# Second attention: scores from stacked high and low halves that transfers put in place

## What is computed

```python
def rmsnorm(x, g):
    xf = x.astype(jnp.float32)
    y = xf * lax.rsqrt(jnp.mean(xf * xf, axis=-1, keepdims=True) + EPS)
    return (y * g.astype(jnp.float32)).astype(x.dtype)
...
def window_attention(q, k, v, k_ctx, v_ctx, sink, scale):
...
        s_ctx = jnp.einsum('bqkgd,bckd->bkgqc', qi, k_ctx).astype(jnp.float32) * scale
        s_win = jnp.einsum('bqkgd,bskd->bkgqs', qi, ki).astype(jnp.float32) * scale
        s_win = jnp.where(valid, s_win, NEG_INF)
        p = jax.nn.softmax(jnp.concatenate([s_ctx, s_win, sink_col], axis=-1), axis=-1).astype(v.dtype)
        return (jnp.einsum('bkgqc,bckd->bqkgd', p[..., :n_ctx], v_ctx)
                + jnp.einsum('bkgqs,bskd->bqkgd', p[..., n_ctx:n_ctx + span], vi))
...
    k_ctx, v_ctx = gqa_keys_values(h_ctx, k_g)
    k_lat, v_lat = gqa_keys_values(h_lat, k_g)
    q_lat = apply_rope(gqa_queries(h_lat, q_g), cos, sin).reshape(B, L, C_KV_HEADS, C_GROUP, C_HDIM)
    k_lat = apply_rope(k_lat, cos, sin)
    o_lat = window_attention(q_lat, k_lat, v_lat, k_ctx, v_ctx, sink, scale)
```

## Time and profile before

| what | value |
|---|---|
| median of 3 runs | 3370.38 us (3369.05 to 3371.79) |
| the profiled execution | 3368.63 us, of which the span is 3366.8 us |
| TensorE busy | 3128.4 us (93%), 14506 instructions |
| VectorE, ScalarE, GpSimd busy | 1618.1 us, 1043.6 us, 472.2 us |
| mean granted clock of TensorE | 0.967 |
| second attention | 2192 to 2513 us of the span |

### The profile page before, as it was taken

How to read it: one execution, slowest core, us unless ns; L and a number is a source line. 1 busy time by engine, 2 the same in 40 slices (tenths; PEclk the granted TensorE clock), 3 DMA queues, 4 the chain that set the end, 5 groups by cost and what they waited for, 6 DMA issues and landing times. The chain is left out here.

```text
span 3366.8 us, 38293 instructions
## 1 busy us (share of the span) xinstructions
PE 3128.4 (93%) x14506; PEld 2220.9 (66%) x14506; DVE 1618.1 (48%) x2027; ACT 1043.6 (31%) x1435; POOL 472.2 (14%) x375
## 2 busy tenths in 40 slices
PE   5987999999897999999999969879989899999998
PEld 2552444444586888888888847734438688888887
DVE  4123555565326555555555462255633555555554
ACT  3014566556413111111111130035552312222221
POOL 0003554555300000000000000035440000000000
PEclk9987999999898999999999989979999899999999
DMA  9800000000201111111111001000000211111111
GB/s 384 328 36 17 4 4 3 2 3 0 94 19 70 38 35 35 36 35 34 36 35 37 25 13 50 25 16 1 1 20 31 76 38 44 62 44 44 44 62 50
DMA packets 34912, 162.28 MB, mean 48 GB/s; under 512 B 3890, under 2 KB 6706, under 8 KB 24755
## 3 DMA queue, kind: packets, MB, share of 16 engines
q1 hardware_dynamic: 34834, 161.24, 13.4%
HBM read 157.03 MB, written 4.19 MB: 48 GB/s over the span
## 5 line engine op out<-in xcount | busy, mean ns | idle before, releaser
L716 PE MATMUL PS<-f_uh,f_Wh 128*128 128x512 f32 (+1 forms) x1760 | 483.4, 372 | 25.2 <-DVE f_ul L453 24.2
L716 PE MATMUL PS<-f_ul,f_Wh 128*128 128x512 f32 (+1 forms) x1760 | 481.7, 371 | 0.0
L716 PE MATMUL PS<-f_uh,f_Wl 128*128 128x512 f32 (+1 forms) x1760 | 480.9, 371 | 0.0
L866 DVE SCALAR_TENSOR_TENSOR X<-PS,mod,X 128x512 f32<-128x512 f32 (+1 forms) x440 | 306.3, 698 | 309.1 <-PE PS L716 308.9
L716 PEld LDWEIGHTS PS<-f_uh,f_Wh 128*128 128x128 f32 x1760 | 307.8, 188 | 89.6 <-issue 19.4
L716 PE MATMUL PS<-f_gh,f_WDh 128*128 128x512 f32 (+1 forms) x880 | 330.8, 376 | 19.4 <-DVE f_gl L852 17.2
L716 PEld LDWEIGHTS PS<-f_ul,f_Wh 128*128 128x128 f32 x1760 | 308.8, 188 | 59.1
L716 PEld LDWEIGHTS PS<-f_uh,f_Wl 128*128 128x128 f32 x1760 | 308.4, 188 | 59.0
L716 PE MATMUL PS<-f_gl,f_WDh 128*128 128x512 f32 (+1 forms) x880 | 325.8, 370 | 0.0
L716 PE MATMUL PS<-f_gh,f_WDl 128*128 128x512 f32 (+1 forms) x880 | 325.7, 370 | 0.0
L835 DVE SCALAR_TENSOR_TENSOR part<-PS,part,part 128x1023 f32<-128x1023 f32 (+1 forms) x132 | 130.0, 1013 | 328.6 <-ACT part L771 328.5
(11 more groups left out here) (268 smaller groups left out, 4601.0 us busy)
## 6 DMA issues: line engine op xcount, KB each, us to landing
part<-in_mod_w SPq DMA_DIRECT2D x48, 1024.0 KB, 7.3
part<-in_w_up SPq DMA_DIRECT2D x88, 512.0 KB, 3.5
part<-in_w_down SPq DMA_DIRECT2D x22, 1024.0 KB, 5.5
part<-in_w_out SPq DMA_DIRECT2D x16, 512.0 KB, 3.5
X<-in_xT SPq DMA_DIRECT2D x4, 1280.0 KB, 10.2
...
```

What stands on the lines that cost most here:

```text
L716: mm = pe.matmul(ps(bank + c, hi - lo), w_, x_[:, lo:hi], start=f_, stop=l_)
L866: dve.scalar_tensor_tensor(out=X[:, m, lo:hi], in0=ps(DNB[r % 2], hi - lo), scalar=moda(layer, 5, m, 0 if lo < SEQ else 1), in1=X[:, m, lo ...
```

## The change

The score product becomes two float32r products into the same bank. `ks` holds the low half of K on the upper 64 partitions and the high half on the lower, `qh` the high half of Q twice, so one pass gives low K with high Q and high K with high Q. `kh` (high K, with the row of ones) times `ql` (low Q, with the row of the maximum) is the second.

VectorE now writes a finished piece over all 128 rows in place into its PSUM bank (L2274; for the context piece one operation, L2262, with no rotation product and no `turn`). In the pair after, ScalarE copies it to a stage as float32r, its high half (`high`, L2155), VectorE subtracts to the low half (`low`, L2282), GpSimd casts the high half to bfloat16 after its addition (L1963), and SyncE moves the parts to their partitions: four transfers of the high half, two of bfloat16, two of the low half for a full piece. The first three pieces and the rest have stages of their own: `high` and `low` wait for the transfers of all pieces before from the fifth piece on, since those share one stage. Squares of the first four pieces use two buffers. Four buffers for queries take the place of six. The zero fills of the bfloat16 tiles go from VectorE to GpSimd, the rotation table comes in four transfers, and TensorE no longer waits for it. Pieces and early maxima stand at other pairs, and upfront the steps of neighbouring pieces interlock.

```diff
-            qa = [[take(SEQ) for _ in range(C_GROUP)] for _ in range(2)]
-            ka = [take(T) for _ in range(2)]
-            pr = [take(2, BANK) for _ in range(3)]
-            osb = take(BANK)
-            acc = [take(SEQ) for _ in range(2)]
-            rope = take(2, T)
-            qb = [take(SEQ // 2).bitcast(BF16) for _ in range(C_GROUP)]
-            kb = [take(T // 2).bitcast(BF16) for _ in range(2)]
-            es = take(SEQ)
-            sq = [take(BANK) for _ in range(2)]
-            lnr = take(BANK)
...
-            t1, lnb = X[:, 0:2, SEQ:T], X[:, 2:4, SEQ:T]
...
+            QS = 4
+            qh, ql = halves("qh", QS, SEQ), halves("ql", QS, SEQ)
+            at_pr = [take(2, BANK) for _ in range(3)]
+            pr = [big(x, 2, BANK) for x in at_pr]
+            rope = [plain(SEQ), MIX1[:, 5, :]]
+            ks, kh = halves("ks", 2, T), halves("kh", 2, T)
+            acc = [plain(SEQ) for _ in range(2)]
+            qb = [plain(SEQ // 2).bitcast(BF16) for _ in range(C_GROUP)]
+            kb = [plain(T // 2).bitcast(BF16) for _ in range(2)]
...
+            sq = [QK1[:, 1:4:2, SEQ:T], acc[1][:, 0:BANK].rearrange("p (a b) -> p a b", b=CTX)]
+            early_b = [acc[0][:, 256 * n:256 * n + 256].bitcast(BF16) for n in range(3)]
+            stages = [(place("h1_stage_h", take(2, CTX), 2, CTX),
+                       place("h1_stage_l", O_QK1, KT, T)[:, 5:8:2, SEQ:T])]
+            for b in range(3):
+                stages.append([place(f"h1_stage_{kind}{b}", at_pr[b] + n * BANK, 2, CTX) for n, kind in enumerate("hl")])
+            t1, lnb, osb = [X[:, 2 * b:2 * b + 2, SEQ:T] for b in range(3)]
+            stage_b = X[:, 6, SEQ:T].bitcast(BF16)
...
+                at(pair - 1, 1 if pair > 1 else 0, "tn", G, w)
                 at(pair, 0, "nt", G, w)
                 at(pair, 1, "ro", G, w)
-                at(pair + 1, 0, "ca", G, w)
+                at(pair + 1, 0, "hi", G, w)
+                at(pair + 1, 1, "lo", G, w)
+                at(pair + 1, 1, "ca", G, w)
+
+            def upfront(n):
+
+                for kind, w in [("sq", 0), ("nt", 0), ("tn", 0)] + [(kind, w + d) for w in range(n) for kind, d in (
+                        ("ro", 0), ("sq", 1), ("nt", 1), ("tn", 1), ("hi", 0), ("lo", 0), ("ca", 0)) if w + d < n]:
+                    at(UPFRONT, 0, kind, 0, w)
...
-            EARLY = [(0, 0), (0, 1), (1, 0), (1, 1), (2, 0), (2, 1), (3, 0), (4, 0)]
+            EARLY = [(0, 0), (0, 1), (1, 0), (1, 1), (2, 1), (3, 0), (3, 1), (4, 0)]
...
-                for w, r in enumerate((-15, -13, -9, -7, -3)):
-                    product(o + r if G else 1 if w == 4 else UPFRONT - 1, G, w)
+                if G == 0:
+                    upfront(NW - 1)
+                    product(0, G, NW - 1)
+                else:
+                    for w, r in enumerate((-15, -13, -10, -7, -3) if G == 1 else (-19, -15, -13, -7, -3)):
+                        product(o + r, G, w)
...
+                def moves(G, w):
+
+                    t_, c = prods[w]
+                    b, lo, hi = G % 2, *CH[c]
+                    top, bottom = slice(0, 64), slice(64, P)
+                    first, second = [], []
+
+                    def query(j, rows_):
+                        n = queries(G, j)
+                        first.extend((qh[n][half, lo:hi], rows_) for half in (top, bottom))
+                        second.append((ql[n][top, lo:hi], rows_))
+                    if t_ == 0:
+                        first.extend(((ks[b][bottom, lo:hi], bottom), (kh[b][top, lo:hi], bottom)))
+                        second.append((ks[b][top, lo:hi], bottom))
+                        if c < 2:
+                            query(2, top)
+                    else:
+                        query(0, top)
+                        query(1, bottom)
+                    return first, second
...
+                def staged(G, w):
+
+                    return stages[w + 1 if G == 0 and w < 3 else 0]
...
+                def before(q):
+
+                    return 0 if q < 4 else q
...
+                    sp.wait_ge(s["one"], 2 + QS)
+                    for G in range(C_KV):
+                        for w in range(NW):
+                            q = NW * G + w
+                            m = CH[prods[w][1]][1] - CH[prods[w][1]][0]
+                            at_least(sp, "S", 2 * NU * (C_GROUP * G + (-3 if w < 3 else -1)))
+                            first, second = moves(G, w)
+                            stage_h, stage_l = staged(G, w)
+                            sp.wait_ge(s["hi"], q + 1)
+                            for dst, rows_ in first:
+                                sp.dma_start(in_halves(dst).bitcast(F32), halved(stage_h[rows_], m).bitcast(F32))\
+                                    .then_inc(s["moved"], 16)
+                            sp.wait_ge(s["cast"], q + 1)
+                            sp.wait_ge(s["pad"], 2 + C_GROUP)
+                            at_least(sp, "mx", 24 * (G - 1) + (8 if w < 3 else 24))
+                            for dst, x in rounding(G, w):
+                                sp.dma_start(dst, x).then_inc(s["rounded"], 16)
+                            sp.wait_ge(s["lo"], q + 1)
+                            for dst, rows_ in second:
+                                sp.dma_start(in_halves(dst).bitcast(F32), halved(stage_l[rows_], m).bitcast(F32))\
+                                    .then_inc(s["moved"], 16)
+                            if q > 1:
+                                sp.wait_ge(s["rounded"], rounded(q + 1))
+                                sp.wait_ge(s["moved"], moved(q + 1))
...
+                    for x in (*kb, *qb):
+                        pool.memset(x[64:P, :], 0.0).then_inc(s["pad"], 1)
+                    for x in ql:
+                        pool.memset(x[64:P, :].bitcast(F32), 0.0).then_inc(s["one"], 1)
+                    pool.wait_ge(s["one"], 2 + QS)
+                    pool.wait_ge(s["pad"], 2 + C_GROUP)
...
+                        m = CH[prods[w][1]][1] - CH[prods[w][1]][0]
+                        q = NW * G + w
+                        pool.wait_ge(s["hi"], q + 1)
+                        at_least(pool, "rounded", rounded(before(q)))
+                        pool.tensor_copy(in_halves(rounded_in(q)[:, 0:m]), halved(staged(G, w)[0], m).bitcast(F32)).then_inc(s["cast"], 1)
...
-                            casts(NU * n + u, 0)
                             add(n, u)
+                            casts(NU * n + u, 1)
...
+                                pe.wait_ge(s["moved"], moved(NW * G + (3 if j == 2 else NW)))
                             ends = [(kt - 1 >= q0 and kt < 8, 0, 0), (kt + 1 < q1 and kt < 8, w - P, 1)]
                             last = [e for e in ends if e[0]]
-                            mm = pe.matmul(ps(i % 3, w), ka[G % 2][:, kt * P:(kt + 1) * P],
-                                           qa[G % 2][j][:, q0 * P:q1 * P], start=True, stop=not last)
+                            q = queries(G, j)
+                            pe.matmul(ps(i % 3, w), ks[G % 2][:, kt * P:(kt + 1) * P], qh[q][:, q0 * P:q1 * P],
+                                      start=True, stop=False)
+                            mm = pe.matmul(ps(i % 3, w), kh[G % 2][:, kt * P:(kt + 1) * P], ql[q][:, q0 * P:q1 * P],
+                                           start=False, stop=not last)
...
-                        at_least(pe, "out", q if q > 3 else max(q - 2, 0))
+                        at_least(pe, "lo", q if q > 3 else max(q - 2, 0))
                         at_least(pe, "fin", done["spread"])
                         nb, tb = banks(G, w)
-                        pe.matmul(ps(nb, hi - lo), bones, sq[q % 2][:, :hi - lo], start=True, stop=True)
-                        pe.matmul(ps(tb, hi - lo), rot1[:, 1 - t_, :], QK1[:, 2 * G + t_, lo:hi],
-                                  start=True, stop=True).then_inc(s["nt"], 1)
+                        m = hi - lo
+                        mm = pe.matmul(in_halves(ps(nb, m)), bones, halved(square_in(q), m), start=True, stop=True)
+                        if c < 2:
+                            mm = pe.matmul(ps(tb, m), rot1[:, 1 - t_, :], QK1[:, 2 * G + t_, lo:hi],
+                                           start=True, stop=True)
+                        mm.then_inc(s["nt"], 1)
...
-                        pe.wait_ge(s["cast"], NW * G + (3 if jj == 0 else 4 if qt < 4 else 5))
+                        pe.wait_ge(s["rounded"], rounded(NW * G + (3 if jj == 0 else 4 if qt < 4 else 5)))
+                        if (G, jj, qt) == (0, 0, 0):
+                            pe.wait_ge(s["lo"], 3)
+                            pe.wait_ge(s["pad"], 2 + C_GROUP)
...
+                    def high(G, w):
+                        m = CH[prods[w][1]][1] - CH[prods[w][1]][0]
+                        q = NW * G + w
+                        act.wait_ge(s["out"], q + 1)
+                        at_least(act, "moved", moved(before(q)))
```

(24 more changed lines are left out.)

123 lines of the change are left out of this document (72 added, 51 removed).

## The result

The kernel after takes 3338.3 us (median of four runs, 3335.9 to 3341.2) where the kernel before, run beside it, takes 3369.7: a ratio of 0.9908, with a 95% interval of 0.9896 to 0.9921. The forecast was 3327 us, with 3314 to 3348 as its range. The gain is 31 us, not 43.

The account below looks back on a forecast made before the run. TensorE's queue was taken to bound the second attention's main loop. Gains of 46 + 2 + 2 less 5.4 and 1.7 us gave 43 us off, so 3327 us; 3314 to 3348 us was to hold 8 in 10.

Parts of the forecast that it names:

- Score products: All 144 score products on TensorE: two float32r passes replace one float32 instruction, 46 us gained, from 44 to 51.
- Waits for the reductions: Maxima in the loop wait for VectorE's reductions, no longer covered by score pairs: 0.45 us a head, 5.4 us lost.
- the cast on GpSimd: First head: TensorE's 1.76 us wait for a cast and the low clock after it shrink, 2 us gained, 0 to 4.
- group 1's third piece: Its transfer lands 5.3 us after pair 9 starts, TensorE wants it at 3.6: 1.7 us lost, 0 to 4.
- the term of the rotation: Where a piece's rotation lies between two reductions on VectorE, the 0.46 us wait grows by some 0.15 us.
- The opening: Stage start: first product some 5 us earlier, spent again on the pieces' chain; 0 us, 3 gained to 4 lost.
- Transfers hidden: A piece's copy, issues and landing in the loop take 5.5 us, hidden within 6.4 us by 0.9 us.
- The clock: Rival 1: each head loses TensorE's full clock once after new waits, 20 us come back, 3347 us; chance 15%.
- (3): Rival: sixteen pieces' transfers through one stage become the loop, slower, 3426 us with 17.5 us landings; chance 4%.
- (4): Rival: score products are not halved, a float32r pass costs 0.43 us like a float32 record, 3368 us; chance 3%.
- (2): Rival: transfers land a little late, five places wait 2.9 us each, 15 us, 3342 us; chance 8%.
- The signs: Expected in the profile: 0.225 us pass distance, heads some 19 us, PEclk 1.00, landing near 2 us, first score product 2224 to 2232.

## Why the prediction was right, and where its sizes were off

**The time** was in the range and 11 us above the forecast. By the stage alone it is 34.5 us of gain where 43 were forecast. Of the 8.5 us between them, 4.8 are in heads 0 and 1, 3 in the ten heads behind, and 0.8 in the opening.

**Score products: 46 us, measured 42.** Two products of 512 columns with what starts them take 1.01 us (2308.32 and three passes of 0.23) where they took 1.77; at 384 columns to the mask 0.44 and not 0.70. By all shapes that is 48 x 0.38 + 72 x 0.27 + 24 x 0.18 = 42 us (0.27 and not 0.26, as the product behind a mask follows it sooner; the 0.18 is read in the same way from the rows of 256 columns). The distances that the forecast took hold for the second pass, 0.23 and 0.18 us; the first pass after other work takes 0.32 and 0.26. That start was in the float32 rows as well, so the difference could not be had from records in mid-row alone. The Trainium skill's rule of four passes for true float32 (FP8 and Floating Point Precision, Matmul Precision) would have given 49; the 46 us by the rows were nearer.

**Waits for the reductions: 0.45 us a head more, measured 0.3.** 42 us are 3.5 a head. Nine heads gained 30.3, and two of the three context pieces of the loop fall into them, 0.6 us each, so 9 x 3.5 + 1.2 - 30.3 = 2.4 us do not show, 0.3 a head. The pass issued twice gives 0.5, but it also covers the wait behind a rotation, which the kernel before had as well: 0.46 us in every third head, 0.41 now. The forecast let it grow by 0.15 us, and it did not; what is new are the 0.07 to 0.16 us behind the score pairs. The mechanism stands, the size was 0.15 us a head too high.

**Heads 0 and 1: a gain of 7 us, measured 2.2.** Here is the step that failed. The forecast gave them their share of the score products, 2 us for the cast on GpSimd, and 1.7 us of loss for group 1's third piece. That one came as forecast, 1.45 us, and the wait of 1.76 us for the cast is gone. But the fifth piece, which the forecast had as "one step later" and free, is waited for by 1.60 us, and two waits for a reduction behind a rotation went from 0.38 and 0.86 to 1.40 and 2.22; the forecast let such a wait grow by 0.15 us. With 0.90 for the finish of a head and the 1.20 that both kernels have, that is 8.8 us of waits against 4.2. Two heads' share of the 42 us is 7.0, and a context piece's rotation gives 0.6, so 7.0 + 0.6 - 4.6 = 3.0 us, where 2.2 were measured. These heads have the low clock for 9.8 us, 6.8 before; that has the size of the 0.8 us left, but no run takes just this away. For the term of the rotation the forecast looked at a steady head, where 1.1 us of value products (L2017) stand between the two maxima in question. Ahead of the wait of 2.22 us nothing stands between them.

**The opening: 0 us, measured a loss of 0.8**, but not by the chain of the forecast. As forecast, TensorE started some 5 us earlier (0.7 us after the start of the stage, 5.8 before), and the last upfront product ended at 18.6 us (20.0 forecast). But the first maximum, which waits for the third piece's bfloat16, started at 26.6 us where the forecast had that piece landed at 24.7, behind SyncE's queue at 0.60 us an issue and not 0.34, which itself began only with the last fill on GpSimd. The forecast named no queue on SyncE for the opening; the runs show it as the bound, with 4.0 us to be had at the first maximum by its order alone, and with ScalarE's earlier copy 8.2 there and 6.5 at the first score product. The 5 us won by not waiting for the table were spent on this queue. The first score product came 36.3 us after the start of the stage where the forecast had 35.2; that it was so near is luck, since the chain that the forecast followed was not the one that bound.

**Transfers hidden: right in the loop, though the chain is longer than forecast.** Eight issues of 0.6 us and 2.3 of landing are 7.1 us, not 5.5. ScalarE's copy is never seen waiting for a transfer in the kernel after. What does not fit is a piece's way to its first maximum: with the old places TensorE waits 4.2 to 6.5 us for it.

**The rivals.** The clock did not fall once a head: it is 1.00 from 2266 to 2484 us, nearly to the end of the stage, across waits of 0.41 us. It fell behind the wait of 2.22 us at the end of head 0 (0.53 in the next 6 us). By the Trainium skill's rule on short idles (TensorE: Matmul & The Clock Gate, PSUM-queue depth-cycling) it might have swung; with one such wait in every third head it did not. The stage as one chain of transfers (3) and a change without halving (4) are ruled out by the rows above. The late transfers of (2) are there in the first two heads alone, by the issue and not the landing.

**The signs** held for the distances of the passes, the clock and the landing, and for the waits of the maxima in steady heads (heads 0 and 1 have up to 2.22 us). Two did not: heads of "some 19 us" are so only on average (177.6 / 9 = 19.7, with 16.7 to 21.4 by their pieces), and the first score product came at 2235.6 us, outside 2224 to 2232, of which 7 us are the late start of that execution's stage.
